# Projections and output projection as three products of high and low parts, with weight pieces in a ring

## The reference

```python
for layer in range(2):
    h = rms_norm(x, attn_norm[layer])
    if layer == 0: mix = hgrn2_diff_mixer(h, ...)   # h @ w_in (1024 x 3584), heads, ... @ w_out (1024 x 1024)
    else:          mix = gla_mixer(h, ...)          # h @ w_in (1024 x 3088), heads, ... @ w_out (1024 x 1024)
    x = x + mix
    h = rms_norm(x, ffn_norm[layer])
    x = x + hierarchical_moe(h, ...)                # 16 experts of 1024 x 512, 1024 x 512, 512 x 1024; top 2 of one group
```

## Time and profile before

| | us |
|---|---|
| Median of 3 runs (1428.44 to 1429.82) | 1428.84 |
| The profiled execution's own time | 1432.67 |
| Its span, first to last instruction | 1430.9 |
| Mixer of layer 0, to its last routing product | about 382 |
| Experts of layer 0 | about 418 to 720 |
| Mixer of layer 1 | about 743 to 1064 |
| Experts of layer 1 | about 1101 to 1403 |

### The profile page before, as it was taken

One profiled execution on the slowest core, in us unless ns is written; L12 is line 12 of the kernel. 1 busy time (PEld: TensorE's weight loads), 2 busy tenths in 40 slices (PEclk: granted clock), 3 DMA queues, 4 the chain that ended last, 5 costly groups with the idle time before them and its releaser, 6 DMA issues.

```text
span 1430.9 us, 15450 instructions
## 1 busy us (share of the span) xinstructions
PE 1266.8 (89%) x5120; PEld 796.0 (56%) x5120; DVE 820.9 (57%) x1201; ACT 602.6 (42%) x760; POOL 92.9 (6%) x131
## 2 busy tenths in 40 slices
PE   5999999989759999999829999998975999999982
PEld 3444456654636766667514446655464666666751
DVE  2325645342548888888631215334353888888872
ACT  2115620011208777777511210011120877777760
POOL 1020000010000000000030000001000000000002
PEclk9999999999659999999959999999975999999995
DMA  7111110321629999999631121040153999999935
GB/s 257 59 59 59 60 59 1 77 62 59 234 99 361 387 388 389 390 390 391 261 129 55 35 91 40 21 123 12 59 193 124 338 389 387 390 390 386 390 115 187
DMA packets 127558, 282.41 MB, mean 197 GB/s; under 512 B 16896, under 2 KB 17408, under 8 KB 127504
## 3 DMA queue, kind: packets, MB, share of 16 engines
q1 hardware_dynamic: 103456, 245.38, 46.5%
q0 software_dynamic: 5888, 20.97, 4.6%
q10 hardware_dynamic: 18160, 15.36, 3.4%
HBM read 262.82 MB, written 18.87 MB: 197 GB/s over the span
## 4 chain that ended last, share of the span: by engine, by line
PE 67%; DVE 14%; issue 10%; ACT 4%; DMA 2%; POOL 2%; ACTq 1%; DVEq 0%; SPq 0%; POOLq 0%
PE PS L1041 24%; PE PS L1193 8%; PE PS L1195 8%; PE PS L1194 8%; DVE expert_w_low L1667 7%; PE PS L1152 6%; PE PS L1064 4%; ACT weight_high L768 1%; PE PS L1164 1%; POOL yg L676 1%; PE PS L996 1%; PE PS L1097 1%; DVE xgT_low L1675 1%; PE PS L1177 1%; DMA x_sb<-in_x 1%
## 5 line engine op out<-in xcount | busy, mean ns | idle before, releaser
L1667 DVE TENSOR_TENSOR expert_w_low<-expert_w,weight_high 128x1024 fp32r<-128x1024 f32 x368 | 426.1, 1220 | 69.5 <-ACT weight_high L768 65.5
L768 ACT ACTIVATE weight_high<-expert_w 128x1024 fp32r<-128x1024 f32 x384 | 374.9, 1048 | 66.2 <-PE PS L1195 58.1
L1041 PE MATMUL PS<-weight_ring,hT 128*128 128x512 f32 x576 | 262.2, 605 | 9.6 <-ACTq L797 8.1
L1193 PE MATMUL PS<-weight_high,xgT_high 128*96 128x512 f32 x512 | 206.5, 403 | 6.3 <-DVEq L1677 3.9
L1195 PE MATMUL PS<-weight_high,xgT_low 128*96 128x512 f32 x512 | 203.8, 398 | 0.0
L1194 PE MATMUL PS<-expert_w_low,xgT_high 128*96 128x512 f32 x512 | 203.5, 397 | 0.0
L1041 PEld LDWEIGHTS PS<-weight_ring,hT 128*128 128x128 f32 x576 | 107.9, 194 | 129.0 <-issue 118.0
L1193 PE MATMUL PS<-weight_high,actT_high 128*96 128x512 f32 x256 | 105.3, 411 | 16.4 <-DVEq L1704 16.2
L1041 PE MATMUL PS<-hT,weight_ring 128*128 128x512 f32 x256 | 114.3, 598 | 1.1 <-ACTq L841 0.9
L1152 PE MATMUL PS<-weight_ring,hT 128*128 128x512 f32 x256 | 111.2, 592 | 0.0
L1193 PEld LDWEIGHTS PS<-weight_high,xgT_high 128*96 128x96 f32 x512 | 83.5, 163 | 41.5 <-DVEq L1677 4.5
(11 more groups left out here) (213 smaller groups left out, 1172.8 us busy)
## 6 DMA issues: line engine op xcount, KB each, us to landing
expert_w<-in_moe_w_gate SPq DMA_DIRECT2D x32, 2048.0 KB, 12.8
expert_w<-in_moe_w_up SPq DMA_DIRECT2D x32, 2048.0 KB, 12.1
expert_w<-in_moe_w_down SPq DMA_DIRECT2D x32, 2048.0 KB, 12.2
weight_ring<-in_even_w_in SPq DMA_DIRECT2D x6, 2048.0 KB, 7.8
y_rows<-yb ACTq DMA_DIRECT2D x32, 384.0 KB, 6.0
weight_ring<-in_odd_w_in SPq DMA_DIRECT2D x6, 2048.0 KB, 9.2
weight_ring<-in_even_w_out SPq DMA_DIRECT2D x2, 2048.0 KB, 8.9
h_rows<-h SPq DMA_DIRECT2D x8, 512.0 KB, 9.6
```

Of the source, the lines that this page charges most:

```text
L768: act_(hi, w, ACT.Copy).then_inc(w_hi, 1)
L1041: ins = pe.matmul(bank(s), a, b, start=k == 0, stop=k == KD - 1)
L1193: pe.matmul(out, ah, bh, start=first, stop=False)
L1667: tt(lo, w, hi.bitcast(F32), ALU.subtract).then_inc(w_lo, 1)
```

## The change

- The weight ring of three buffers is replaced by two raw buffers of 2 MB (`raw`) and a ring of six pieces of high parts (`g_hi`, 0.5 MB each). A group has four pieces of two k each. A new step `split` makes one: ACT copies it to the rounded type (`g_hi`), DVE writes the low part over the raw weights.
- Each float32 product of the projections, of `wo` and of alpha is now three products (`three`).
- `hT` and `oT`, where the projections read them, become `hTh` and `hTl`: ACT copies both halves, DVE subtracts both. The rows for the routing stay float32.
- `with_splits` puts a group's first two splits right after the third unit of the group before it (`proj` or `wo` with u = 2), and the last two just ahead of that group's fourth unit, which is now always in halves where it is a projection. The first group's splits stand in `norm_steps`: in layer 0 behind the first `hT`, in layer 1 ahead of everything.
- The order of the start changes a little in `norm_steps`: in layer 0, `hT` 0 no longer stands behind the square of rows 2.
- SP loads a group when the group two before is used up. The first experts' loads wait for other buffers: gate 0 for the last `out`, up 0 and gate 1 for the last units of the two output groups as before; down 0 and up 1 no longer wait for the routing.
- The memory is laid out anew; `wgt` is written over `prob`; the mask `reset`, which nothing read, is gone, and the clearing of AT moves from the constants (layer 0) and from alpha (layer 1) to behind `cum`.

```diff
+        u = [("proj", n // 2, MIX[n // 2][0][0], i) for i in range(NT)]
+        own = [("split", n // 2, 0, q) for q in range(4)]
+        if n == 0:
+            return [x[0], x[1], h[0], h[1], hT[0], *own, halves[0], hT[1], x[2], h[2], u[0], hT[2], x[3], h[3], u[1],
+                    hT[3], u[2], halves[3], u[3]]
+        return [*own, x[0], x[1], h[0], x[2], h[1], hT[0], halves[0], x[3], h[2], hT[1], u[0], h[3], hT[2], u[1],
+                hT[3], u[2], halves[3], u[3]]
...
+    def with_splits(l, steps):
...
+        for s in steps:
+            unit = s[0] in ("proj", "wo")
+            if unit and s[3] == NT - 1:
+                out += [k for k in next_group(s)[2:] if k]
+            out.append(s)
+            if unit and s[3] == NT - 2:
+                out += [k for k in next_group(s)[:2] if k]
...
         def _(sp):
             def load_group(n, src):
-                place_free(n)
-                sp.dma_start(wbuf[:, n % 3], src).then_inc(w_loaded[n % 3], 16)
+                if n - 2 in reader:
+                    bk.wait_full(sp, reader[n - 2])
+                sp.dma_start(raw[n % 2][:], src).then_inc(w_loaded[n % 2], 16)
@@ -773,6 +793,22 @@
+                    elif kind == "split":
+                        g, q = first_group[l] + s[2], s[3]
+                        n, w, hi, _ = piece(g, q)
...
+                        if g and q >= 2:
+                            sc.wait_ge(piece_done, 2 * (g - 1) + q - 1)
+                        act_(hi, w, ACT.Copy).then_inc(g_hi_ready, 1)
...
+                            for g in range(2):
+                                bk.wait_full(sc, (*s, g))
+                                act_(hTh[:, 4 * g:4 * g + 4, cols], bank((*s, g)).rearrange("p (k n) -> p k n", k=4),
+                                     ACT.Copy).then_inc(hTh_ready, 1)
@@ -974,6 +1016,14 @@
+            def three(out, pairs, first, final):
+                (ah, al), (bh, bl) = pairs
+                pe.matmul(out, ah, bh, start=first, stop=False)
+                pe.matmul(out, ah, bl, start=False, stop=False)
+                return pe.matmul(out, al, bh, start=False, stop=final)
...
-                            ins = pe.matmul(bank(s), a, b, start=k == 0, stop=k == KD - 1)
+                            if u == 0 and k % 2 == 0:
+                                pe.wait_ge(g_lo_ready, 4 * g + k // 2 + 1)
...
+                            ins = three(bank(s), pairs, k == 0, k == KD - 1)
+                            if u == NT - 1 and k in (1, 3):
+                                ins.then_inc(piece_done, 1)
@@ -1390,17 +1425,32 @@
+                        if in_parts(s):
+                            for g in range(2):
+                                r = slice(4 * g, 4 * g + 4)
+                                ve.wait_ge(hTh_ready, 2 * parts_no[s] + g + 1)
+                                link(tt(hTl[:, r, cols], bank((*s, g)).rearrange("p (k n) -> p k n", k=4),
+                                        hTh[:, r, cols].bitcast(F32), ALU.subtract))
+                                ve.sem_inc(bk.freed((*s, g)), 1)
+                            ve.sem_inc(hT_v, 1)
...
+                    elif kind == "split":
+                        g = first_group[l] + s[2]
+                        n, w, hi, lo = piece(g, s[3])
+                        ve.wait_ge(g_hi_ready, n + 1)
+                        tt(lo, w, hi.bitcast(F32), ALU.subtract).then_inc(g_lo_ready, 1)
```

More of the change, by code:

```diff
@@ L145, in mixer_steps @@
                 if n < 6:
-                    steps += stats + [unit] + dT
+                    steps += stats + (halves[unit] if unit[3] == NT - 1 else [unit]) + dT
                 else:
@@ L159, in mixer_steps @@
         else:
-            steps += ([("alpha", l)] + units[4:6] + [("alpha2", l)] + units[6:9] + [("fx", l)] + units[9:12]
-                      + [("cum", l)])
+            steps += ([("alpha", l)] + units[4:6] + [("alpha2", l), units[6]] + halves[units[7]] + [units[8], ("fx", l)]
+                      + units[9:11] + halves[units[11]] + [("cum", l)])
             rest = units[12:]
@@ L202, in norm_steps, with next_group @@
     def norm_steps(n):
[L203 to L220, removed]
+        u = [("proj", n // 2, MIX[n // 2][0][0], i) for i in range(NT)]
+        halves = [("half", *k[1:]) for k in u]
+        x, h, hT = ([(kind, n, i) for i in range(NT)] for kind in ("x", "h", "hT"))
+        own = [("split", n // 2, 0, q) for q in range(4)]
[5 more added lines that the diff above has]
+    def with_splits(l, steps):
+        names = [k for k, _ in MIX[l]]
+        out = []
+        def next_group(s):
+            g = names.index(s[2]) if s[0] == "proj" else len(names) + s[2]
+            return [("split", l, g + 1, q) for q in range(4)] if g < len(names) + 1 else [()] * 4
+        for s in steps:
[5 more added lines that the diff above has]
+                out += [k for k in next_group(s)[:2] if k]
+        return out
+    STEPS = [with_splits(l, norm_steps(2 * l) + mixer_steps(l)) for l in range(NL)]
     NBK = [NH * dv // GC for dv in DVS]
@@ L286, in build @@
         arena = cursor[0]
[L288 to L301, removed]
@@ L1151, in _ @@
                         for k in range(KD):
-                            ins = pe.matmul(bank(s), hT[:, k, i * P:(i + 1) * P], wbuf[:, g % 3, k, :],
-                                            start=k == 0, stop=k == KD - 1)
+                            if i == 0 and k % 2 == 0:
+                                pe.wait_ge(g_lo_ready, 4 * g + k // 2 + 1)
+                            rows = slice(i * P, (i + 1) * P)
+                            ins = three(bank(s), ((hTh[:, k, rows], hTl[:, k, rows]), group_k(g, k)), k == 0, k == KD - 1)
+                            if i == NT - 1 and k in (1, 3):
+                                ins.then_inc(piece_done, 1)
                         ins.then_inc(bk.filled(s), 1)
@@ L1187, in _ @@
                     ins.then_inc(bk.filled(key) if k == 2 * NT - 1 else idx_step, 1)
-                def three(out, pairs, first, final):
-                    (ah, al), (bh, bl) = pairs
-                    pe.matmul(out, ah, bh, start=first, stop=False)
-                    pe.matmul(out, ah, bl, start=False, stop=False)
-                    return pe.matmul(out, al, bh, start=False, stop=final)
                 def wait_low(pos, b, part):
```

223 lines of the change are left out of this document (120 added, 103 removed).

## The result

| | us |
|---|---|
| before, median of 4 runs on this chip | 1428.64 (1426.84 to 1429.82) |
| changed kernel, median of 4 runs | 1418.06 (1417.23 to 1418.72) |
| ratio after / before | 0.9927 (95% interval 0.991 to 0.9944) |
| profiled execution after | 1418.72, span 1417.0, mean granted clock 0.907 (before 0.933) |

What follows compares the result with a forecast made beforehand. The mixers were taken as bound by PE, with DVE and ACT not far behind in places. Of 89.1 us gross, 60.2 were lost, leaving 28.9 gained: about 1400 us from 1428.84, taken as 1401, range 1374 to 1424.

Steps and rivals of the forecast that it cites:

- Pace: Projection products with 128 stationary columns keep the experts' 0.2314 us; a unit takes 5.56 us instead of 6.87, 89 us gross.
- Rival B: The new products run at the pace of float32's pairs, 0.215 us: 1375 us; chance 8%.
- Rival D: Slower than before, as the load of 128 columns isn't hidden, 0.262 us a product: 1436 us; chance 7%.
- The three long waits: Levels: PE waits 7.3 us behind v's third unit in layer 0, v2's and g's in layer 1; 21.9 us lost.
- The clock: PE runs slower after idling: 2.3 us lost behind each of the three long waits, 6.9 us.
- Attention: Differential attention: waits from splits lose 13 us, all of the gross gain there; range 5 to 20 us.
- Start: Start of layer 0: the four dv units go from 48.9 to about 43.9 us, 0.2 us lost in waits.
- Layer 0's outputs: First `wo` splits delay DVE's sum to t+6.5 from t+1.6, 4.9 us lost; another 1.3 us not gained.
- Layer 1: Losses of 0.5 us at `hT`, 1.3 at k's first piece, 2.6 in g2; alpha's own gain gone.
- Rival A: The splits hide on DVE and ACT, idle 43% and 58% of the span: 1347 us; chance 5%.
- Rival C: Waits smaller by a third, in attention and with a warm clock: 20 us less, 1381 us; chance 17%.
- Rival E: More waits in attention and behind the levels, or pace 0.237: 10 to 20 us more, 1410 to 1420; chance 18%.

Runs made afterwards that it cites:

- experiment 1: Changed kernel with a group's first two splits just ahead of the third unit's last step instead of behind it: 1382.0 us, ratio 0.9642.
- experiment 3: Changed kernel loading and splitting only 8 of 512 columns, except each layer's first two groups; order kept, result wrong: 1385.89 us, ratio 0.9681.
- experiment 7: experiment 4 with only 8 of 512 columns loaded and split, except each layer's first two groups: 1350.82 us, ratio 0.943.
- experiment 2: Changed kernel with 28 unused products on PE in each of the three long waits in the levels: 1407.15 us, ratio 0.9823.
- experiment 4: Kernel of experiment 1 with ACT issuing the parameter transfers of `inter` a few at a time in the levels: 1371.46 us, ratio 0.9575.
- experiment 5: Kernel of experiment 1 with DVE's constants in four portions in dq's sums and the start's parameter transfers behind dq's last high part: 1382.56 us, ratio 0.9652.
- experiment 6: Kernel of experiment 1 with the edits of experiment 4 and experiment 5 together: 1373.98 us, ratio 0.9593.
- experiment 9: experiment 4 with the parts of w_a made behind q's parts in layer 1, not in `alpha`: 1368.95 us, ratio 0.9564.
- Experiment 8: Changed kernel with only the parameter transfers moved into the levels, splits left where they are: 1411.37 us, ratio 0.987.
- experiment 10: experiment 9 with the two splits of a pair put in two separate places wherever a unit comes in halves: 1385.5 us, ratio 0.9674.

## Why the prediction was right, and where it was wrong

**Pace: right.** 0.2295 us in a row and 0.233 over a whole unit (5.60/24) with 128 columns; unit 5.60 us for 5.56. Rivals B and D are out: the load of 197 ns stays hidden, and 0.215 is not reached. That last figure is nearly what the Trainium skill gives, page "TensorE: Matmul & The Clock Gate", section "Back-to-back issue gap", N / 2.4 + 2.5 ns, 216 ns for 512 columns; the trace disagrees with it for this type by 14 ns.

**The three long waits: right.** 7.03 + 7.61 + 7.04 = 21.7 us for 21.9, each ended by the update of K behind two low parts; experiment 1 removes them by the order alone. The waits of the second splits came too, 0.55, 0.89 and 0.55 us for 2.4. What I did not draw from my own sum is what experiment 3 splits off: 4.1 of 7 us are the position behind an eviction, with put and update behind it, and would be there with almost no work in the splits.

**The clock: wrong, and the step that failed.** I counted 2.3 us behind each of the three long waits, 6.9 us, and nothing behind any other wait. The same products take, beside experiment 7, where PE never waits in the levels, 64.91-57.30 = 7.6 us more in layer 0 and 75.72-68.35 = 7.4 us more in layer 1. That is 15.0 us in the levels, where I had 6.9. Experiment 2 gives some 11 of them back with the waits for DVE kept. Two things were wrong in the term. Its price was too low: my own case, PE's return after 4.96 us of idle time, held 1.4 us on the half unit and 1.8 us on the small products before it, 3.2 us, and I charged 2.3; the trace has 1.7 us on the level and 1.9 on the half unit, 3.6. That is 3.9 of the 8.1 us that are missing in the levels. And I charged the clock only behind the long waits: in layer 0 there are 1.51 and 1.10 us waits at the start of the levels, and 0.55 and 0.89 us ones later, and the granted clock is 0.55 from 203.81 to 207.61 and 0.52 from 256.21 to 258.84. Such waits do not always do this: experiments 1, 4, 5, 6 and 9 have the same ones in this stretch, and it took 61.0 us at a clock of 1.00 in experiment 4 and 63.9 in the other four (0.95 in experiments 1 and 9). The kernels differ in what goes ahead of the stretch; why one of them stays at the full clock is not shown.

The page says the same of the whole kernel. The terms of my sum other than the clock are 60.2-6.9 = 53.3 us of waits, and PE's idle time grew by 52.6. PE's busy time was to fall by 89.1-6.9 = 82.2 us, and fell by 66.5. So by these busy times the waits were right in their sum, and all of the shortfall stands in products that ran slower than I said, with the pace at the full clock as forecast.

**Attention: the sum right, its parts wrong.** Nothing was gained, as said. But 13 us of waits were forecast, and the idle time grew only from 105.11-97.15 = 8.0 to 105.88-89.46 = 16.4 us. Its nine and a half units should have brought PE's busy time from 97.15 to 84.7; it is 89.46, 4.8 us of clock that I had not charged. The two errors cancel, so that the sum came out is luck. With the clock of the levels and attention at 19.8 us instead of 6.9 and the waits at 8.5 instead of 13, these two terms explain 8.4 of the 15.3 us that are missing.

**Start: too good by 2.1 us.** dq's group begins at 46.05, not 43.9. ACT issues the eight parameter transfers (27.85 to 33.3) ahead of the last transposed block's high part, so DVE's constants run 2 us later than I had them, and PE waits 2.56 us. I had the transfers' arrival in the sum, not the place they take in ACT's queue. Behind that wait the gaps are 0.43 us from 47.4 to 50.4, which costs about 1.5 us more; the stage up to dk's third unit gained 1.3 us less than forecast.

**Layer 0's outputs: the size right, the cause half right.** Counted from the eviction's end t, the state's copy was forecast to end at t+5.8 and the sum at t+6.5; the trace has 6.0 and 6.9. But most of PE's 9.01 us wait is not the splits, as I wrote, but the 8 us of issued transfers (eleven, not ten) in front of them, which before had the same place and mattered less. Experiments 4 and 8 leave the splits and bring this wait and the next together from 9.6 (experiment 1) to 2.6 and from 10.4 to 4.6 us; experiment 3 takes the splits' work out, leaves the transfers and still has 7.6 us.

**Layer 1: too good by 5 us**, 1.6 of it before its levels and 3.5 in and behind them. The wait for w_a's parts was there as foretold (1.71 us). The rest is the clock again, and 2.3 us of waits at the first outputs: 4.16 and 1.69 us ahead of the second state product and behind it, where the kernel before has one of 3.58. I had said that this stage comes out where it was. Experiment 8, with the transfers moved, has 1.48 and 2.52 us there, so they are about 1.9 us of it.

**Rival A** said that the splits hide; experiments 1 and 7 bound it. Placed well they still cost some 20 us with their transfers, placed as in the change 36 us more. **Rival C** is half seen: attention's waits were a third smaller, but the clock, which it took for full, was what failed. **Rival E** has the time in its range, 1410 to 1420, but not its reason: it was neither more idle time in all than I counted nor the pace.

## What to carry to other kernels

When work is given to engines that are half idle, its place in their order counts more than its length: put it ahead of the step whose input it would delay, never right behind an eviction that waits for TensorE, and count all that the queue holds there, issued transfers too. Charge a new wait of TensorE of 2 us and more with more than its idle time: the clock behind it mostly slows what runs next here, small products as well, by half of the idle time again behind waits of 7 us (experiment 2: 11 us behind 21.7) and by more than the idle time behind waits of 2 to 3 (experiment 10). To price the clock apart from the wait, fill the wait with unused products and time that.

## What the hardware showed that I had not expected

Three waits of 2 to 3 us went with more loss in clock than in time: in experiment 10, 7.5 us more idle time came with 11.8 us more busy time for the same products, some of it behind smaller waits. At the lower of its two levels TensorE takes 0.43 us for a product that takes 0.23 at the upper, and the levels' small products with their loads of 128 columns double too. The Trainium skill describes this in the page "TensorE: Matmul & The Clock Gate", section "HAM oscillation — how this bites in real kernels": a wait for data lets the clock fall and the next tile starts cold, each time. The traces agree, with 3.6 us behind a 7 us wait for another engine. And 28 unused products in each of three waits made a kernel 11 us faster.
